# Gate products of a recurrent unit: three fp32r products in place of one fp32 product each

## The reference, cut to what matters

```
u = causal_depthwise_conv(u, conv_w, conv_b)          # 4 taps
ub = u.reshape(B, S, 16, 64)
r = sigmoid(einsum('bshi,hij->bshj', ub, w_rg) + b_rg)
i = sigmoid(einsum('bshi,hij->bshj', ub, w_ig) + b_ig)
log_a = -8 * r * softplus(-lru_lambda)
a = exp(log_a);  xin = sqrt(-expm1(2 * log_a)) * (i * u)
h_t = a_t * h_{t-1} + xin_t                           # a scan over the tokens
y_b = (h * silu(g_lru)) @ w_pb
```

## Time and profile before

| | us |
|---|---|
| median of 3 runs | 2901.51 (2901.15 to 2901.82) |
| the profiled execution, its own time | 2899.96 |
| its span, first to last instruction | 2898.2 |
| PE busy in the span | 2828.0 (98%) |
| DVE busy | 1722.5 (59%) |
| ACT busy | 1308.5 (45%) |
| POOL busy | 729.3 (25%) |

### The profile page before, as it was taken

The page is one execution under the profiler, slowest core; times in us unless marked ns, Lnnn a source line. Parts: engine busy times, 40 slices in busy tenths (PEclk is TensorE's granted clock), DMA queues, the critical chain, the costliest instruction groups (busy, mean ns, idle before and its releaser), DMA issues. The chain is left out here.

```text
span 2898.2 us, 34915 instructions
## 1 busy us (share of the span) xinstructions
PE 2828.0 (98%) x13286; PEld 2320.9 (80%) x13286; DVE 1722.5 (59%) x1877; ACT 1308.5 (45%) x1537; POOL 729.3 (25%) x279
## 2 busy tenths in 40 slices
PE   7999999989999999999999999999999999999999
PEld 6887888648888888888888877888988777778887
DVE  7962112688888888888888875041311423874132
ACT  4232003357777777777777754030212311333021
POOL 0002322002222222222333322312222233333230
PEclk9999999999999999999999999999999999999999
DMA  4021113499999999999999972111111411111131
GB/s 161 23 56 47 44 44 136 164 362 363 384 385 385 384 380 382 383 380 384 382 384 383 382 269 104 49 52 51 55 55 45 147 44 58 44 44 44 51 124 58
DMA packets 127075, 555.98 MB, mean 192 GB/s; under 512 B 14545, under 2 KB 22753, under 8 KB 93825
## 3 DMA queue, kind: packets, MB, share of 16 engines
q1 hardware_dynamic: 116160, 523.91, 47.8%
q0 software_dynamic: 5328, 20.07, 2.5%
q10 hardware_dynamic: 5490, 10.62, 1.0%
HBM read 521.42 MB, written 32.09 MB: 191 GB/s over the span
## 5 line engine op out<-in xcount | busy, mean ns | idle before, releaser
L2494 DVE TENSOR_TENSOR slots_lo<-buffer,slots_hi 128x2048 fp32r<-128x2048 f32 x384 | 851.6, 2288 | 105.9 <-ACT slots_hi L1788 105.9
L1788 ACT ACTIVATE slots_hi<-buffer 128x2048 fp32r<-128x2048 f32 x384 | 709.2, 1951 | 40.2 <-PE bank L1305 29.1
L1002 PE MATMUL bank<-hT_hi,ring_hi 128*128 128x512 f32 x1216 | 483.4, 398 | 9.9 <-POOL ring_lo L909 6.1
L1004 PE MATMUL bank<-hT_hi,ring_lo 128*128 128x512 f32 x1216 | 474.4, 390 | 0.0
L1003 PE MATMUL bank<-hT_lo,ring_hi 128*128 128x512 f32 x1216 | 474.1, 390 | 0.0
L961 POOL DMA_INDIRECT xacc<-buffer x15 | 276.4, 18425 | 622.1 <-ACT buffer L1856 622.1
L906 POOL CAST ring_hi<-buffer 128x1024 fp32r<-128x1024 f32 x101 | 114.8, 1137 | 849.6 <-DMA buffer<-in_wstream 849.6
L909 POOL TENSOR_TENSOR ring_lo<-buffer,ring_hi 128x1024 fp32r<-128x1024 f32 x111 | 283.4, 2555 | 51.1 <-ACT ring_hi L1538 43.0
L1002 PEld LDWEIGHTS bank<-hT_hi,ring_hi 128*128 128x128 f32 x1216 | 228.8, 188 | 62.1 <-DVE hT_lo L2603 7.1
L1004 PEld LDWEIGHTS bank<-hT_hi,ring_lo 128*128 128x128 f32 x1216 | 228.5, 188 | 48.4
L1003 PEld LDWEIGHTS bank<-hT_lo,ring_hi 128*128 128x128 f32 x1216 | 228.9, 188 | 46.0 <-issue 1.2
(11 more groups left out here) (495 smaller groups left out, 4029.0 us busy)
## 6 DMA issues: line engine op xcount, KB each, us to landing
buffer<-in_w_gate SPq DMA_DIRECT2D x128, 1024.0 KB, 7.7
buffer<-in_w_up SPq DMA_DIRECT2D x128, 1024.0 KB, 4.9
buffer<-in_w_down SPq DMA_DIRECT2D x128, 1024.0 KB, 7.9
buffer<-in_wstream SPq DMA_DIRECT2D x154, 512.0 KB, 3.5
buffer<-in_x SPq DMA_DIRECT2D x16, 512.0 KB, 8.5
od<-buffer ACTq DMA_DIRECT2D x24, 260.0 KB, 2.1
xacc<-buffer SPq DMA_DIRECT2D x8, 512.0 KB, 2.8
h2d<-buffer SPq DMA_DIRECT2D x8, 512.0 KB, 4.8
```

The source lines that it names most:

```text
L1002: mm(bank, lhs[0], rhs[0], start=first, stop=False)
L1004: return mm(bank, lhs[1], rhs[0], start=False, stop=last)
L1788: fn(slots_hi[:, n_ % NH, :], slots[n_ % NS], ACT.Copy).then_inc(slot_high_ready, 1)
L2494: tt2(slots_lo[:, place_of(n_), :], slots[n_ % NS], slots_hi[:, n_ % NH, :].bitcast(F32), ALU.subtract).then_inc(slot_split, 1)
```

## The change

The gate products become `three_passes` too. For that the weights `rgig` and the input `uc` are split. ACT copies `rgig` to `rgig_hi` once, before the loop; DVE makes `rgig_lo` after `convolve(0)`. In each step ACT copies each half of `uc` to `uc_hi`, and DVE subtracts to `uc_lo` in `convolved_low(c)`, directly after `convolve(c)`. `uc_hi` lies where `ra` goes afterwards and `uc_lo` where `ii` goes. `uc_ready` now counts halves. The semaphores of yl's split and of this one are joined to `lru_high_ready` and `lru_split`; PE's gate products wait for `lru_split` half by half.

On ACT the copies of block c stand after the Silus of block c-2 in the queue, so the order in a step is Silu, Silu, Copy, Copy for 2q, and the same for 2q+1. The Sigmoid of lr waits until li is full too. On DVE the order is `convolve(2q)`, `convolved_low(2q)`, `convolve(2q+1)`, `convolved_low(2q+1)`, and only then the two `output`.

```diff
+        rgig_hi = part("rgig_hi", 46 * K, 8, 2, P)
+        rgig_lo = part("rgig_lo", 48 * K, 8, 2, P)
+        uc_hi = part("uc_hi", 6 * K, 2, SEQ)
+        uc_lo = part("uc_lo", 14 * K, 2, SEQ)
...
-                if q == 0:
-                    pe.wait_ge(rgig_loaded, 16)
                 if q < 4:
                     for c in (2 * q, 2 * q + 1):
-                        pe.wait_ge(uc_ready, c + 1)
                         for h in range(2):
+                            pe.wait_ge(lru_split, 1 + 2 * c + h + 1)
+                            hs = slice(h * HALF, (h + 1) * HALF)
                             for name, j in (("lr", 0), ("li", 1)):
                                 bank = b2.wait_free(pe, (name, c, h))
-                                mm(bank[:], rgig[:, c, j, :], uc[:, c % 2, h * HALF:(h + 1) * HALF],
-                                   start=True, stop=True).then_inc(full2, 1)
+                                three_passes(bank[:], (rgig_hi[:, c, j, :], rgig_lo[:, c, j, :]),
+                                             (uc_hi[:, c % 2, hs], uc_lo[:, c % 2, hs]), True, True).then_inc(full2, 1)
...
-                    pe.wait_ge(yl_split, 8)
+                    pe.wait_ge(lru_split, 17 + 8)
...
+            act.wait_ge(rgig_loaded, 16)
+            fn(rgig_hi.rearrange("p a b c -> p (a b c)"), rgig.rearrange("p a b c -> p (a b c)"), ACT.Copy).then_inc(
+                lru_high_ready, 1)
             for q in range(5):
-                if q > 0:
-                    for c in (2 * q - 2, 2 * q - 1):
-                        for h in range(2):
-                            bank = b2.wait_full(act, ("lg", c, h))
-                            fn(yl[:, c, h * HALF:(h + 1) * HALF], bank[:], ACT.Silu).then_inc(drained2["act"], 1)
+                for c in (2 * q, 2 * q + 1):
+                    for h in range(2 if q > 0 else 0):
+                        bank = b2.wait_full(act, ("lg", c - 2, h))
+                        fn(yl[:, c - 2, h * HALF:(h + 1) * HALF], bank[:], ACT.Silu).then_inc(drained2["act"], 1)
+                    for h in range(2 if q < 4 else 0):
+                        hs = slice(h * HALF, (h + 1) * HALF)
+                        act.wait_ge(uc_ready, 2 * c + h + 1)
+                        fn(uc_hi[:, c % 2, hs], uc[:, c % 2, hs], ACT.Copy).then_inc(lru_high_ready, 1)
...
-                        bank = b2.wait_full(act, ("lr", c, h))
+                        b2.wait_full(act, ("li", c, h))
+                        bank = b2.bank(("lr", c, h))
                         if q:
                             act.wait_ge(yl_ready, c - 1)
...
+            def convolved_low(c):
+
+                for h in range(2):
+                    hs = slice(h * HALF, (h + 1) * HALF)
+                    dve.wait_ge(lru_high_ready, 1 + 2 * c + h + 1)
+                    tt2(uc_lo[:, c % 2, hs], uc[:, c % 2, hs], uc_hi[:, c % 2, hs].bitcast(F32), ALU.subtract).then_inc(
+                        lru_split, 1)
...
                 for c in pair:
                     convolve(c)
+                    if c == 0:
+                        dve.wait_ge(lru_high_ready, 1)
+                        tt2(rgig_lo.rearrange("p a b c -> p (a b c)"), rgig.rearrange("p a b c -> p (a b c)"),
+                            rgig_hi.bitcast(F32).rearrange("p a b c -> p (a b c)"), ALU.subtract).then_inc(lru_split, 1)
+                    convolved_low(c)
                 if q:
                     for c in pair:
                         output(c - 2)
```

More of the change, by code:

```diff
@@ L599, in build_program @@
         att_high_ready, att_split = sem("att_high_ready"), sem("att_split")
-        yl_high_ready, yl_split = sem("yl_high_ready"), sem("yl_split")
+        lru_high_ready, lru_split = sem("lru_high_ready"), sem("lru_split")
         merged2_high_ready, merged2_split = sem("merged2_high_ready"), sem("merged2_split")
@@ L1988, in _ @@
                         fn(ra[:, c % 2, hs], bank[:], ACT.Sigmoid, bias=col("b_rg", c)).then_inc(drained2["act"], 1)
-                        bank = b2.wait_full(act, ("li", c, h))
+                        bank = b2.bank(("li", c, h))
                         fn(ii[:, c % 2, hs], bank[:], ACT.Sigmoid, bias=col("b_ig", c)).then_inc(drained2["act"], 1)
@@ L2002, in _ @@
             for c in range(8):
-                fn(yl_hi[c // 4][:, c % 4, :], yl[:, c, :], ACT.Copy).then_inc(yl_high_ready, 1)
+                fn(yl_hi[c // 4][:, c % 4, :], yl[:, c, :], ACT.Copy).then_inc(lru_high_ready, 1)
             for f in range(8):
@@ L2772, in convolve @@
                         step(stt(o, ubuf[:, 3 - i:3 - i + HALF], tap(i), o, ALU.mult, ALU.add))
+                    stt(o, ubuf[:, 0:HALF], tap(3), o, ALU.mult, ALU.add).then_inc(uc_ready, 1)
+                    dve.wait_ge(uc_ready, 2 * c + h + 1)
                     if h == 0:
-                        step(stt(o, ubuf[:, 0:HALF], tap(3), o, ALU.mult, ALU.add))
                         step(v.tensor_copy(ubuf[:, 0:3], ubuf[:, HALF:HALF + 3]))
-                    else:
-                        stt(o, ubuf[:, 0:HALF], tap(3), o, ALU.mult, ALU.add).then_inc(uc_ready, 1)
-                        dve.wait_ge(uc_ready, c + 1)
+            def convolved_low(c):
[4 more added lines that the diff above has]
+                        lru_split, 1)
             def output(c):
@@ L2805, in _ @@
             for c in range(8):
-                dve.wait_ge(yl_high_ready, c + 1)
-                tt2(yl_lo[:, c, :], yl[:, c, :], yl_hi[c // 4][:, c % 4, :].bitcast(F32), ALU.subtract).then_inc(yl_split, 1)
+                dve.wait_ge(lru_high_ready, 17 + c + 1)
+                tt2(yl_lo[:, c, :], yl[:, c, :], yl_hi[c // 4][:, c % 4, :].bitcast(F32), ALU.subtract).then_inc(lru_split, 1)
             def merged2_low(f):
```

## The result

The changed kernel takes 2909.15 us (median of 13 runs, 2906.47 to 2911.35), the kernel before beside it 2901.73 (13 runs, 2900.49 to 2904.83). The ratio is 1.0025, with a 95% interval of 1.0017 to 1.0032: 7.4 us slower, more than the 0.2% (5.8 us) that the prediction counts as a difference, though the interval begins a little under it. The forecast was 2907.8 us, slower. The profiled run took 2907.81 us, with a span of 2906.0, 7.8 us more than before.

A forecast was written before the change was run, and what follows sets the result against it. PE was taken to bound this stage. Step 0 +5.4 us, clock +1.6 and steps 1 to 3 -0.7 sum to +6.3, carried onto the median 2901.5 for 2907.8 us; range +2.3 to +9.5, 2903.8 to 2911.0.

The forecast's parts named there:

- What is saved: Gate products on PE: three passes take 0.68 us instead of 0.859, saving 1.43 us a step.
- The port: DVE instructions on two SBUF operands and POOL's split exclude each other; whoever waits gets the next turn.
- rival 1: Step 0: uc_lo(0) gets the port ahead of POOL's subtraction; +3.9 or +2.5 us, 2904.0 to 2905.8; chance 0.27.
- rival 2: The port does not matter for the new instructions at all; -4.1 us, 2897.4; chance 0.06.
- Step 0: First gate stage: PE idles 7.4 us for DVE's uc_lo and ends the gates 5.4 us later, saving counted in.
- The clock: After the wait in step 0 PE runs at half clock for a while; 1.6 us lost, bounds 0 and 2.9.
- Steps 1 to 3: Later gate stages: gates gain 2.6 us, bank waits cost 2.0, so 0.7 gained in all.
- the term for the bank: After each later step's gates PE waits 0.45 plus 0.2 us for ACT's Sigmoid of lr to free a bank.
- The end: Split of yl before B(0): no cost, 2.5 us of slack left.
- The sum: Whole kernel: +5.4 + 1.6 - 0.7 = +6.3 us, giving 2907.8 us.
- rival 3: Late scans delay the next convolution, or yl's split delays B(0); +9 to +12 us, 2911 to 2913; chance 0.13.
- Rival 4: Gate products: three passes miss the streaming rate and stay at the old 0.86 us each; +12 us; chance 0.02.

The follow-up runs named there:

- e5_copies: Changed kernel with ACT making the high parts of uc ahead of the Silus; 2902.16 us in one run, steps 1 to 3 48.96 us each.
- e1_pool: Changed kernel with POOL's splits of two weight tiles held back until uc_lo stands; PE's wait in step 0 4.09 us instead of 7.03, step 0 11.42 instead of 14.36.
- e2_clock: Changed kernel with 30 overwritten matmuls filling PE's wait in step 0; step 0 12.96 us instead of 14.36, total 2909.85 us.
- e9_fill: e8_all with ten overwritten matmuls in PE's wait in step 0; 2899.08 us against 2902.60 for the kernel before, ratio 0.9986.
- e4_table: Changed kernel with a one-column Sigmoid after ACT's last copy, loading the table early; steps 1 to 3 49.26 us each, step 0 14.34.
- e7_rgig: Changed kernel with rgig loaded early and rgig_lo made ahead of convolve(0); wait 5.43 us, step 0 13.31, total 2910.2 us.
- e8_all: Changed kernel with the edits of e1_pool, e5_copies and e7_rgig together; 2900.19 us against 2902.79 for the kernel before, ratio 0.9990.
- e3_output: Changed kernel with DVE's output(2q-2) put ahead of uc_lo(2q); steps 1 to 3 49.23, 49.44 and 49.31 us, step 0 14.41.

## Why the prediction was right, and where it wasn't

**What is saved: right.** A product takes 0.68 us, and a step without waits 48.96 (e5_copies), 1.44 less than 50.40; forecast 1.43.

**The port: right in mechanism and sizes.** `rgig_lo` was forecast with a record of 3.0 us and has 3.02, the first `uc_lo` with 2.8 and its longest record is 2.87, and the waiting engine got the next turn each time, which was the ground for putting rival 1 below the forecast. By e1_pool the port is worth at least 2.9 us of the wait, and rival 2, under which it is worth nothing, is refuted.

**Step 0: right.** The forecast was 5.4 + 1.6 = 7.0 us lost, measured 6.86. The wait was 7.03 instead of 7.4, for the gates began 0.8 us later than before and `convolve(0)` ended 0.8 us later too (2443.83 against the 2443.05 of the earlier trace rows), so both moved together, and the links between came out 0.2 to 0.4 shorter than forecast.

**The clock: right.** Forecast 1.6; measured 4.45 - 2.89 = 1.6 by e2_clock, and 4.45 - (2461.05 - 2458.20) = 1.6 by e9_fill. The reason given for the lower value, that time at the low level passes inside a wait as long as this one, fits the changed kernel, where the clock was down from 2457.3 (worked out from the window at 0.66) and PE restarted at 2460.71. That the figure came out exact is luck in part: after waits of 5.4 to 7.3 us the four products took from 4.18 us (e4_table) to 5.00 (e7_rgig), so 1.3 to 2.1 lost, and e8_all lost 1.6 with none of the low stretch inside its wait.

**Steps 1 to 3: the step that failed.** Forecast 0.7 gained, measured 0.2 lost (0.1 by the steps in the table, 0.22 to B(0)). A step was to take 49.5 to 50.2 us and took 50.44. The gates' part was about right: PE reached the second block at 2511.65, 2.97 us after 2508.68 instead of 2.72, and needed 0.16 more to get going, 0.41 in all against the forecast 0.55. Wrong was the term for the bank. It was put at 0.65, and PE stood from 2514.53 to 2515.60, 1.07 us, with about 0.1 for the restart. Two errors lie in it, of opposite sign. I let POOL's CAST go ahead of `output(2q-2)`, which would then end at G+5.75. In fact DVE was at the port 0.01 us before it (2512.18 against 2512.19), and the output was done at about G+4.7 (G is 2508.68 here). And I let the Sigmoid start right behind the output, leaving out that ACT needs the Sigmoid's table between Silu and Sigmoid, and that this load waits where the Sigmoid waits. I had counted tables only for the new copies, which indeed need none. With the load in its right place and the CAST in the wrong one the forecast would have been a wait of 1.9 us, and steps of 50.40 - 1.43 + 0.55 + 1.9 = 51.4. e4_table shows the load's part: 50.44 - 49.26 = 1.2 us a step. The two rows at the port, both `output` of DVE and POOL's CAST:

```profile
2512.18 3.19 DVE L2799 TENSOR_TENSOR buffer<-buffer 128x1024 f32<-128x1024 f32 x2
```

```profile
2512.19 2.11 POOL L910 CAST ring_hi<-buffer 128x1024 fp32r<-128x1024 f32 x1 [7.32 <-DMA buffer<-in_wstream]
```

The second half of that step, that the late outputs push the next step by nothing or a few tenths, held: the three steps are equal to 0.02 us.

**The end: right.** No wait ahead of B(0), with more slack than the 2.5 us that were forecast: the eight `yl_lo` end at 2654.7 and B(0) starts at 2660.12, 5.4 us later. DVE's row after, to be set against the earlier trace rows:

```profile
2643.42 11.29 DVE L2828 TENSOR_TENSOR yl_lo<-buffer,yl_hi 128x1024 fp32r<-128x1024 f32 x8 [1.13 <-ACT yl_hi L2013]
```

**The sum.** Forecast +6.3 on the profiled run, measured 2907.81 - 2899.96 = +7.85: 0.9 more for steps 1 to 3, 0.1 less for step 0, and 0.78 from ahead of the stage, which no term of the forecast covers. By the medians it is +7.4 against +6.3, and the interval of the ratio holds the 7.08 us up to B(0) and the forecast alike. The price of rival 3 doesn't follow from its rule: two or three further POOL subtractions of 2.25 us on +6.3 give +10.8 to +13.1, not +9 to +12; only how much of this rival lies inside the range hangs on it. Rivals 1 and 2 are refuted by the turns at the port and by e1_pool. Rival 3 did not occur in the places it named, though a wait longer than forecast in steps 1 to 3 is its kind. Rival 4 is refuted by 0.68 us a product.

What stays open: why the four products after the waits of 5.4 to 7.3 us took between 4.18 and 5.00 us, and why the first gate product comes up to 5 us earlier or later from one kernel here to the next, though no edit but that of e7_rgig, which e8_all and e9_fill contain, touches anything far ahead of it.

## What to carry to other kernels

A product made cheaper on the bounding engine pays only if its new operands are made as early as its old ones were: write down for each step when the engine will ask, and follow the new links of the helper engines to that moment, with the port's turns and the function tables in them. Where the engine before it can do the new work earlier at no price (a copy ahead of a Silu, a weight's low part in idle time), that order belongs to the change; here it decided between +7.4 and -2.6 us, the second with POOL's two splits held back too. A table load stands behind the wait of the instruction that it serves, so an engine that idles in that wait should be given something harmless of the coming table first.

## What the runs showed of the hardware that I had not expected

**An operation with one tensor from SBUF is held too.** I had written of operations on two SBUF operands. This one has a single tensor from SBUF, and two columns of scalars beside it. In e8_all, in the timelines of DVE and of POOL:

```profile
2448.02 2.73 DVE L2789 TENSOR_SCALAR buffer<-buffer 128x512 f32<-128x512 f32 x1
...
2454.07 0.55 DVE L2789 TENSOR_SCALAR buffer<-buffer 128x512 f32<-128x512 f32 x1
```

```profile
2448.07 2.39 POOL L917 TENSOR_TENSOR ring_lo<-buffer,ring_hi 128x1024 fp32r<-128x1024 f32 x1
```

The same instruction takes 0.55 us undisturbed and 2.73 beside POOL's subtraction, and ends 0.29 us after it. The Trainium skill has this ("SBUF — State Buffer", "Who interferes with whom"): `tensor_scalar` can enter a mode in which it takes both ports, and then excludes GpSimd. The trace agrees that it is held; in which mode it ran no row shows. The 16 copies out of a bank in `convolve` take 0.69 us each, in the changed kernel and in e8_all alike, and none was held.

**A short wait costs the clock as much as a long one.** After idle times of 2.42, 4.09 and 7.03 us the same four products took 4.45 us, against 2.85 to 2.89 at the full clock; after 5.43 us 5.00, and after 7.26 and 7.27 us 4.27 (e3_output), 4.57 (e5_copies) and 4.18 (e4_table). The length of the wait does not order them. In e8_all and e1_pool the clock fell only when PE was at work again. After the waits of 0.9 us in steps 1 to 3 of the changed kernel it stayed at 1.00. The wait of 2.42 us in e8_all thus cost 4.0.

**A table load costs 1.28 us and no more.** In e5_copies a copy ends at 2495.71, the load starts at 2495.73 and the Silu at 2497.02:

```profile
2495.08 0.63 ACT L1992 ACTIVATE uc_hi<-buffer 128x512 fp32r<-128x512 f32 x1 [5.57 <-DVE buffer L2787]
2495.73 1.28 ACT L1988 ACT_TABLE_LOAD   x1
2497.02 1.09 ACT L1988 ACTIVATE buffer<-bank 128x512 f32<-128x512 f32 x2
```

The Trainium skill ("ScalarE: Activation LUTs", "What ACT_TABLE_LOAD costs") gives 1283 ns for the load and 1380 ns for a drain with it, 2.66 us for every switch. The trace agrees with the first figure and has no room for the second: from the end of the copy to the start of the Silu it is 1.31 us.
